# A mixture-of-experts router whose first logits, prefix sums and first gather are placed earlier

## The reference, cut to what matters

```
h2 = rms_norm(x, g_ffn[l])
logits = (h2 @ w_router)                       # 256 x 8
top_val, top_idx = lax.top_k(logits, 2)
gates = one_hot(top_idx) * softmax(top_val)    # summed over the two
for e in range(8):
    y = y + gates[:, e] * (silu(h2 @ w_gate[e]) * (h2 @ w_up[e])) @ w_down[e]
x = x + y                                      # w_gate[e], w_up[e]: 1024 x 3584
```

## Time and profile before

| | |
|---|---|
| median of 3 runs | 1537.99 us (1536.88 to 1538.17) |
| the profiled execution, its own time | 1537.91 us |
| its span, first to last instruction | 1536.1 us |
| PE busy | 1474.5 us (96%) |
| DVE busy | 1090.8 us (71%) |
| ACT busy | 907.7 us (59%) |
| mean granted clock of TensorE | 0.988 |

### The profile page before, as it was taken

The page is one execution under the profiler, slowest core; times in us unless marked ns, Lnnn a source line. Parts: engine busy times, 40 slices in busy tenths (PEclk is TensorE's granted clock), DMA queues, the critical chain, the costliest instruction groups (busy, mean ns, idle before and its releaser), DMA issues.

```text
span 1536.1 us, 16565 instructions
## 1 busy us (share of the span) xinstructions
PE 1474.5 (96%) x6513; PEld 1143.5 (74%) x6513; DVE 1090.8 (71%) x1248; ACT 907.7 (59%) x1206; POOL 68.9 (4%) x102
## 2 busy tenths in 40 slices
PE   7999999998999789999999999999999999999997
PEld 4665688885665467888888888888888888888885
DVE  1344544542244269988998889898898899888894
ACT  2243434431333158777777777787777787777772
POOL 1021000001021001000000000000000000000000
PEclk9999999999999889999999999999999999999999
DMA  8620364528040349999999999999999999999982
GB/s 317 244 110 0 130 226 170 207 92 340 2 164 0 134 157 394 377 368 389 368 372 378 378 354 383 387 365 372 380 356 375 391 361 373 386 353 369 397 333 84
DMA packets 180403, 435.24 MB, mean 283 GB/s; under 512 B 5536, under 2 KB 10336, under 8 KB 180192
## 3 DMA queue, kind: packets, MB, share of 16 engines
q1 hardware_dynamic: 177264, 423.11, 74.5%
q0 software_dynamic: 3056, 11.02, 1.8%
HBM read 428.33 MB, written 5.78 MB: 283 GB/s over the span
## 4 chain that ended last, share of the span: by engine, by line
PE 90%; DVE 6%; ACT 2%; issue 1%; POOL 0%; SPq 0%; DMA 0%; DVEq 0%; ACTq 0%
PE ps L965 13%; PE ps L967 13%; PE ps L966 13%; PE ps L862 8%; PE ps L864 8%; PE ps L863 8%; PE ps L636 8%; PE ps L839 3%; PE ps L840 3%; PE ps L838 3%; PE ps L759 2%; DVE unit_rounded L1609 2%; PE ps L847 2%; PE ps L618 1%; PE ps L730 1%
## 5 line engine op out<-in xcount | busy, mean ns | idle before, releaser
L1609 DVE TENSOR_TENSOR unit_rounded<-wmem,unit_rounded 128x1024 fp32r<-128x1024 f32 (+1 forms) x744 | 854.2, 1210 | 85.9 <-ACT unit_rounded L1174 85.4
L1174 ACT ACTIVATE unit_rounded<-wmem 128x1024 fp32r<-128x1024 f32 (+1 forms) x744 | 719.5, 1042 | 126.2 <-PE ps L967 63.0
L862 PE MATMUL ps<-unit_rounded,vbuf_rounded 128*128 128x512 f32 x536 | 212.8, 397 | 4.5 <-DVE unit_rounded L1609 3.0
L864 PE MATMUL ps<-unit_rounded,stage_rounded 128*128 128x512 f32 x536 | 212.4, 396 | 0.0
L863 PE MATMUL ps<-unit_rounded,vbuf_rounded 128*128 128x512 f32 x536 | 212.4, 396 | 0.0
L965 PE MATMUL ps<-unit_rounded,qkT_rounded 128*128 128x512 f32 x448 | 179.8, 401 | 2.4 <-DVE qkT_rounded L1753 2.4
L965 PE MATMUL ps<-unit_rounded,hT_rounded 128*128 128x512 f32 x448 | 177.2, 395 | 0.0
L967 PE MATMUL ps<-unit_rounded,qkT_rounded 128*128 128x512 f32 x448 | 177.0, 395 | 0.0
L966 PE MATMUL ps<-unit_rounded,qkT_rounded 128*128 128x512 f32 x448 | 176.9, 395 | 0.0
L967 PE MATMUL ps<-unit_rounded,hT_rounded 128*128 128x512 f32 x448 | 174.6, 390 | 0.0
L966 PE MATMUL ps<-unit_rounded,hT_rounded 128*128 128x512 f32 x448 | 174.5, 390 | 0.0
(11 more groups left out here) (210 smaller groups left out, 1322.0 us busy)
## 6 DMA issues: line engine op xcount, KB each, us to landing
wmem<-in_w_exp_gate_dram SPq DMA_DIRECT2D x56, 2048.0 KB, 9.1
wmem<-in_w_exp_up_dram SPq DMA_DIRECT2D x56, 2048.0 KB, 9.6
wmem<-in_w_exp_down_dram SPq DMA_DIRECT2D x56, 2048.0 KB, 9.5
wmem<-in_w_in_dram SPq DMA_DIRECT2D x4, 3072.0 KB, 17.6
wmem<-in_w_ff_gate_dram SPq DMA_DIRECT2D x5, 2048.0 KB, 9.2
wmem<-in_w_ff_up_dram SPq DMA_DIRECT2D x5, 2048.0 KB, 8.3
wmem<-in_w_ff_down_dram SPq DMA_DIRECT2D x5, 2048.0 KB, 9.1
wmem<-in_w_out_dram SPq DMA_DIRECT2D x4, 2048.0 KB, 19.0
```

What stands on the lines that cost most here:

```text
L862: pe.matmul(o, hhb, hi[:, b, c], start=(first and b == 0), stop=False, skip_group_check=True)
L864: mm = pe.matmul(o, hlb, hi[:, b, c], start=False, stop=(b == blocks - 1), skip_group_check=True)
L1174: act.activation(quarter_r(HIGH[l][kind], q, cols), quarter(SETS[l][i][kind], q, cols), ACT.Copy).then_inc(hi_ready[kind], 1)
L1609: dve.tensor_tensor(quarter_r(u, q, cols), quarter(u, q, cols), quarter_r(HIGH[l][kind], q, cols), ALU.subtract).then_inc(lo_ready[kind], 1)
```

## The change

On PE, the first tile's logits stand in front of the second tile's transposes. The five matmuls of the prefix sums become three: one for columns 0 to 15 with both tiles' masks, one that adds the first tile's mask to columns 8 to 15 and 16 to 23 at once, one that adds the second tile's to columns 16 to 23. Only the first has `start=True`. The gather for expert 0 stands in front of the branch, and the first half step waits for each low copy by itself.

On DVE, the selection for expert 0 stands in front of the last two steps of the router, and the low part of the first up matrix and of the tokens in front of the branch. On ACT, the high part of the first up matrix and the rounded tokens stand in front of the branch and no longer wait for the count. The path for all tokens is rearranged to fit.

```
@@ tensor
             attention(1)
-            second_norm(1)
-            second_ready(1)
-
             pe.wait_ge(s_wr, 16)
             for t in range(NT):
+                if t:
+                    second_norm(1)
+                    second_ready(1)
                 for k in range(KD):
                     mm = pe.matmul(ps[:, 0, t * E:(t + 1) * E], hT[:, k, t * P:(t + 1) * P], wr[:, k, :],
                                    start=(k == 0), stop=(k == KD - 1))
             mm.then_inc(r_pe, 1)
 
             pe.wait_ge(r_dve, R_MASK)
-            pe.matmul(ps[:, 1, 0:E], up[:, 0:P], mask[:, 0, :], start=True, stop=True)
-            pe.matmul(ps[:, 1, E:2 * E], up[:, P + 1:2 * P + 1], mask[:, 0, :], start=True, stop=False)
-            pe.matmul(ps[:, 1, E:2 * E], up[:, 0:P], mask[:, 1, :], start=False, stop=True)
-            pe.matmul(ps[:, 1, 2 * E:3 * E], up[:, P + 1:2 * P + 1], mask[:, 0, :], start=True, stop=False)
-            pe.matmul(ps[:, 1, 2 * E:3 * E], up[:, P + 1:2 * P + 1], mask[:, 1, :], start=False, stop=True).then_inc(r_pe, 1)
-            pe.wait_ge(r_dve, R_ALL)
+            every = up[:, P + 1:2 * P + 1]
+            both = mask[:].rearrange("p a e -> p (a e)")
+            pe.matmul(ps[:, 1, 0:2 * E], up[:, 0:P], both, start=True, stop=False, skip_group_check=True)
+            pe.matmul(ps[:, 1, E:3 * E].rearrange("p (a e) -> p a e", e=E), every, mask[:, 0:1, :].broadcast_to([P, 2, E]),
+                      start=False, stop=False, skip_group_check=True)
+            pe.matmul(ps[:, 1, 2 * E:3 * E], every, mask[:, 1, :], start=False, stop=True, skip_group_check=True) \
+                .then_inc(r_pe, 1)
...
-                if kind == 0 and s == 0:
+                if kind == 0 and s == 0 and e:
                     pe.wait_ge(gx_dve, e * KD + KD)
                 for k in range(KD):
+                    if kind == 0 and m == 0:
+                        pe.wait_ge(gx_dve, k + 1)
...
             def slots_path():
-                gather(0)
...
+            gather(0)
+            pe.wait_ge(r_dve, R_ALL)
             by_most(pe, slots_path, tokens_path)
@@ scalar
             act.activation(em[:], dm[:], ACT.Exp).then_inc(r_act, 1)
-            act.wait_ge(r_dve, R_ALL)
...
             def slots_path():
-                high(1, 0, 1, DENSE_STEPS, DENSE_STEPS // 2)
-                gather_high(0)
...
+            high(1, 0, 1, DENSE_STEPS, DENSE_STEPS // 2)
+            gather_high(0)
+            act.wait_ge(r_dve, R_ALL)
             by_most(act, slots_path, tokens_path)
@@ vector
                 done(dve.tensor_scalar(slot[:], slot[:], -1.0, None, ALU.add))
+                select(0)
                 done(dve.tensor_reduce(most[:], ps[:, 1, NT * E:(NT + 1) * E], AX.X, ALU.max))
                 done(dve.tensor_copy(cmax[:], most[:]))
...
             def slots_path():
-                select(0)
-                low(1, 0, 1, DENSE_STEPS)
-                gather_low(0)
...
+            low(1, 0, 1, DENSE_STEPS)
+            gather_low(0)
             by_most(dve, slots_path, tokens_path)
```

More of the change, by code:

```diff
@@ L1014, in tokens_path @@
                 pe.wait_ge(all_low, 1)
+                pe.wait_ge(gx_dve, KD)
                 def expert(pair, p, e, first_step, use):
@@ L1254, in tokens_path @@
             def tokens_path():
+                act.wait_ge(gx_dve, KD)
                 act.activation(xh_r, hT[:], ACT.Copy).then_inc(all_high, 1)
@@ L1258, in expert, with first_of_next @@
                 def expert(pair, p, e, first_step, use):
-                    high(1, p, 1, first_step, use)
                     all_tokens(1, EXPERT_STEPS, first_step, use, p)
-                    next_expert(act, pair, p,
-                                lambda: high(1, 1 - p, 0, first_step + EXPERT_STEPS, use + (EXPERT_STEPS + p) // 2))
+                    def first_of_next():
+                        for kind in range(2):
+                            high(1, 1 - p, kind, first_step + EXPERT_STEPS, use + (EXPERT_STEPS + p) // 2)
+                    next_expert(act, pair, p, first_of_next)
                 pairs(act, expert)
+            high(1, 0, 1, DENSE_STEPS, DENSE_STEPS // 2)
+            gather_high(0)
+            act.wait_ge(r_dve, R_ALL)
             by_most(act, slots_path, tokens_path)
@@ L1634, in all_tokens, with select @@
                 steps(dve, one, n, first_step, use, parity)
+            def select(e):
+                iota = con[:, C_IOTA:C_IOTA + P]
+                for t in range(NT):
+                    at, gate = slot[:, t, e:e + 1], gates[:, t, e:e + 1]
+                    ins = dve.tensor_scalar(sel[:, t, :], iota, at, None, ALU.is_equal)
+                    if e + 1 == E:
+                        ins = dve.tensor_scalar(selg[:, t, :], iota, at, gate, ALU.is_equal, ALU.mult)
+                ins.then_inc(sel_ready, 1)
             def router():
@@ L1698, in _ @@
             router()
[L1700 to L1708, removed]
             def row_numbers(e):
@@ L1807, in expert @@
                 def expert(pair, p, e, first_step, use):
-                    low(1, p, 1, first_step)
                     all_tokens(1, EXPERT_STEPS, first_step, use, p)
@@ L1815, in expert, with first_of_next @@
                                                      in1=xt, op0=ALU.mult, op1=ALU.add).then_inc(x_added, 1)
-                    next_expert(dve, pair, p, lambda: low(1, 1 - p, 0, first_step + EXPERT_STEPS))
+                    def first_of_next():
+                        for kind in range(2):
+                            low(1, 1 - p, kind, first_step + EXPERT_STEPS)
+                    next_expert(dve, pair, p, first_of_next)
                 pairs(dve, expert)
+            low(1, 0, 1, DENSE_STEPS)
+            gather_low(0)
             by_most(dve, slots_path, tokens_path)
```

## The result

The changed kernel takes 1527.75 us (median of 6 runs, 1526.45 to 1530.42), the kernel before 1538.09 us beside it. The ratio is 0.9933 with a 95% interval of 0.9922 to 0.9944, a gain of 8.6 to 12.0 us. The profiled execution took 1526.45 us with a span of 1524.6.

What follows compares the result with a forecast made beforehand. PE, busy 96% of the span, was taken as the bound, with its waits in the router as the room for gain. Terms of 3.49, 0.86, 1.40 and 1.40 sum to 7.15 us: 1537.91 to 1530.8 us, range 1528.0 to 1533.0.

Steps and rivals of the forecast that it cites:

- First term: Router on PE: the first tile's logits go into the 4.47 us gap before the second tile's transposes, -3.49 us.
- Second term: Router's prefix sums on PE: three matmuls for five, wider columns costing nothing, -0.86 us.
- Third term: DVE, first slot instruction to gather: selection before the count, 0.95 us for 2.35, -1.40 us.
- Fifth term: Gather's end to first expert matmul: 2.35 us of read-out go, 0.95 us of branch on PE comes, -1.40 us.
- The bound of nothing: Branch on PE: lower bound of its cost, if PE's sequencer reads the count while matmuls are still queued; upper 1.57 us.
- the branch hides: Rival, PE behind the gather: sequencer runs through the branch during the gather, 1529.8 us; chance 0.27.
- Fourth term: Gather for expert 0 on PE: stays at 5.88 us, with the first low copy ending inside it.
- are the same for this purpose: Whole kernel before: profiled execution, 1537.91 us, and median of the runs, 1537.99, treated as equal.
- faster transposes: Second tile's transposes at full clock, 1.09 us for 1.94; with hidden branch and part of the logits, 1528.0 us.
- the clock did not stay up: Rival, router on PE: logits in the gap keep the clock at 1.00, 1528.2 to 1529.9 us; chance 0.15.
- the gain was not lost to the weights: Rival, expert steps: weight loads set the pace, time stays within 1 us of 1537.9; chance 0.10.
- the path for all tokens, forecast at 2470 us: Rival, prefix sums: old bank contents push the count over 128, every engine takes the slower path; chance 0.03.

Runs made afterwards that it cites:

- e1: Kernel before, with only the first tile's logits moved in front of the second tile's transposes; 1533.37 us beside 1538.73 for the kernel before.
- e2: Changed kernel with all logits put back behind the second tile's transposes; 1532.35 us.
- e4: Changed kernel in which PE waits for the end of its own gather before reading the count; 1531.26 us, ratio to before 0.9948.
- e11: Kernel before run again without an edit; 1535.56 us.
- e3: Changed kernel in which the first half step again waits for all eight low copies; 1532.25 us, ratio to before 0.9956.
- e8: Kernel before with six unread 128-column matmuls filling PE's gap behind the gather; 1537.43 us, ratio to before 0.9998.
- e6: Changed kernel with seven unread matmuls filling PE's four waits in the router; 1525.73 us, ratio to before 0.9917.
- e9: As e6, but five unread 256-column matmuls for the three of 512 in the wait for the mask; 1526.48 us, ratio to before 0.9918.

## Why the prediction was wrong

It was right in direction and in its first three terms, and wrong in size. The step that failed is the charge for the branch on PE; beside it the prediction took one execution's profile for all of them.

- *First term, -3.49:* the prefix sums start 14.25 us into the router for 17.78, 3.53 less. The first logits lay wholly in the gap (e1, e2: 3.53 and 3.5).
- *Second term, -0.86:* from the first prefix matmul to the slot instruction 1.57 us for 2.42, -0.85. Sixteen columns cost what eight do.
- *Third term, -1.40:* 0.96 us for 2.35, -1.39.
- *Fifth term, -1.40, the step that failed:* for the branch the prediction took "0.95, the same sequence measured on the queue where it does lie on the path". PE's sequencer was through it while the gather ran, and the term was -2.35. e4 puts the cost back by making the sequencer wait: +1.2 us. The bound of nothing and the rival "the branch hides" had this case, which the Trainium skill's queue of 64 instructions (Advanced Engine Details and Errata, Engine Queue Depths) spoke for. The trace agrees that the sequencer gets ahead of its matmuls, with the read at 541.0 us against the gather's end at 543.38; how long the queue is no run here shows.
- *Fourth term, 0:* the gather took 5.57 us for 5.89, because the clock rose 3.7 us into it for 4.3, and the first expert matmul's record overlaps its end by 0.17. With the fifth term this is the stretch from the gather's start to the first expert matmul: 5.40 us for 8.26, -2.86 for the -1.40 forecast.

The sum by these measurements is 3.53 + 0.85 + 1.39 + 2.86 = 8.63 us, which is the router's 8.64. It gives 1529.3 us, which still lies in the range; the hidden branch alone had its place there. What took the time below it are the 1.5 us between 1529.3 and 1527.75, and these the terms of the sum don't hold. Here the prediction's sentence failed that the profiled execution and the median "are the same for this purpose": their times were equal, but the stretches inside were not those of every execution. Two things are shown about it. The head was 4.4 us longer in one profile of the changed kernel than in another, the tail of the kernel before 1.5 us (the table; over all kernels they spread by 5.3 and 1.7), so the 2.86 us by which the first two profiles differ there are no gain. And the kernel before has a second price in its router that its profile did not show: the clock held in the 2.35 us gap there, but fell in it in e1 and in e11, at 1.4 us each behind the gap, and the gather in front of it took 0.3 and 0.2 us longer. The changed kernel has no such gap, and its router stayed at 27.86 to 28.07 us in three profiles, where that of before was 36.71 and 38.30. Four profiles have this gap unfilled (before, e1, e3 and e11), and the clock fell in two of them; by that count, an estimate from four executions, the price is 0.8 us on the average, about half of the 1.5. That it is a part of the rest is likely, that it is all of it is not shown; e8 was too small a measurement for either. Nor is the rest clear of noise: the gain's interval of 8.6 to 12.0 us just reaches down to the router's 8.64. The lower end of the range, 1528.0, needed faster transposes beside the hidden branch; they did not come, and that 1527.75 lies so near it is luck.

Of the other rivals: the clock did not stay up through the first logits (transposes 1.98 us), the expert steps kept their 911.2 us, so the gain was not lost to the weights, and the path for all tokens, forecast at 2470 us, was not taken.

## What to carry to other kernels

A move in front of a wait is worth what the profile's chain shows and the chance that the clock falls in the wait as well; compare several executions before a single one's clock goes into a sum. A register load and a branch cost PE nothing if enough matmuls in front of them are still to run, and a microsecond if it must first wait for them: put them behind a batch, with no wait on its end. The batch must be long enough; here the load began when 15 of 32 records had started, and load and branch took about a microsecond. And cut both kernels at the same events before comparing, since here the head, where nothing was changed, differed by 4.4 us between two executions of the changed kernel, half of the router's gain.

## What the runs showed of the hardware

- PE's sequencer read a count from memory 2.4 us before the end of a gather of 32 records that stood in front of it in program order, and 3.0 us after the count was there, when 15 of the 32 had begun. It was 14 or 15 in each of the profiles counted, with the clock at 0.50 or at 1.00.
- Behind the same 8-column matmuls, with PE 100% busy, the clock fell in e6 and stayed at 1.00 in e9; in the kernel before it stood at 0.50 through 6.98 us of them. Eight of them take 1.85 us at the high clock and 3.57 at the low one.
- The same wait of 2.3 us behind the same gather left the clock at 1.00 in one execution and at 0.50 in another (before and e11), and a wait of 3.04 us in front of the last down projection did the same (the changed kernel and before).
- After 2.6 us of idle time PE began the transposes 0.04 us behind the rows that they waited for; in the kernel before, after 4.5 us, 0.25 us behind.
